# Two transformer blocks in one program: the indexer's matmuls interleaved with the projections, relu kept in PSUM, a row sum in another form, and some fillers and weight roundings moved

## The reference

```python
# first block: one input projection, then two attentions
h = rmsnorm(x, g_pre);  proj = h @ w_in        # qa ka va gate_a qi ki wi qb kb vb fb gate_b
# [indexer] scores of all keys, 128 best kept per query
dots  = einsum('bqhd,bsd->bqhs', qi, ki)
score = einsum('bqhs,bqh->bqs', relu(dots), wi)          # 8 heads, causal mask
_, sel = top_k(score, 128)
# [dsa] softmax attention of qa over the selected keys ka, va
# [fox] attention of qb over kb, vb with a bias from cumsum(log_sigmoid(fb)), causal
out = (sigmoid(h @ w_merge)_a * (att_a*silu(gate_a)) @ w_branch_a
     + sigmoid(h @ w_merge)_b * (att_b*silu(gate_b)) @ w_branch_b) @ w_out
x = x + rmsnorm(out);  x = x + rmsnorm(sigmoid(x @ w_ple_gate) * (p @ w_ple))
# second block
# [swa] 8 heads, 2 kv heads, window of 128 keys, a sink in the denominator:
m = maximum(max(s), sink);  p = exp(s - m);  denom = sum(p) + exp(sink - m)
# [mla] latent attention: q from a 384-wide latent (w_uq), k and v from a 256-wide one (w_ukv)
x = x + (sigmoid(g_a)*(o_a @ w_o_swa) + sigmoid(g_b)*(o_b @ w_o_mla)) @ w_out
x = x + (silu(h @ w_gate) * (h @ w_up)) @ w_down;  return rmsnorm(x)
```

## Time and profile before

| | us |
|---|---|
| median of three runs (lowest, highest) | 1259.21 (1259.14, 1259.68) |
| the profiled execution, its own time | 1259.51 |
| its span in the trace | 1257.7 |
| PE busy | 1206.5 (96%) |
| DVE busy | 636.8 (51%) |
| ACT busy | 540.8 (43%) |
| POOL busy | 532.8 (42%) |
| mean granted clock of PE | 0.989 |

### The profile page before, as it was taken

The page is one execution under the profiler, slowest core; times in us unless marked ns, Lnnn a source line. Parts: engine busy times, 40 slices in busy tenths (PEclk is TensorE's granted clock), DMA queues, the critical chain, the costliest instruction groups (busy, mean ns, idle before and its releaser), DMA issues.

```text
span 1257.7 us, 15767 instructions
## 1 busy us (share of the span) xinstructions
PE 1206.5 (96%) x5874; PEld 1000.5 (80%) x5874; DVE 636.8 (51%) x1484; ACT 540.8 (43%) x967; POOL 532.8 (42%) x284
## 2 busy tenths in 40 slices
PE   9989899999999989699988999999999999999997
PEld 8868678788888878499877777788788888888886
DVE  5499575684537274874874585763412222230003
ACT  6443573476523354445763476423432222231112
POOL 1436554344443434134252585444244444424441
PEclk9999999999999999799999999999999999999999
DMA  8303662302322422133112301423323232323221
GB/s 265 101 1 118 172 180 68 101 1 77 119 91 93 144 99 99 34 137 120 34 39 67 101 1 35 174 94 102 99 90 111 69 106 94 101 101 112 84 89 67
DMA packets 71114, 119.18 MB, mean 95 GB/s; under 512 B 5624, under 2 KB 33144, under 8 KB 70656
## 3 DMA queue, kind: packets, MB, share of 16 engines
q1 hardware_dynamic: 71040, 118.19, 28.8%
HBM read 107.67 MB, written 4.21 MB: 89 GB/s over the span
## 4 chain that ended last, share of the span: by engine, by line
PE 80%; DVE 10%; issue 3%; ACT 3%; POOL 2%; SPq 1%; DMA 1%; DVEq 0%; ACTq 0%; POOLq 0%
PE bank L1607 61%; PE bank L1890 9%; PE bank L1688 2%; PE bank L1656 2%; PE bank L1732 2%; DVE sc L1334 2%; PE bank L1670 2%; DVE m L1330 2%; PE bank L1632 1%; DVE tmp L1396 1%; DMA w_raw<-in_w_in 1%; POOL w_lo L652 1%; POOL w_lo L669 1%; SPq L585 1%; SPq L586 0%
## 5 line engine op out<-in xcount | busy, mean ns | idle before, releaser
L652 POOL TENSOR_TENSOR w_lo<-w_raw,w_hi 128x2048 fp32r<-128x2048 f32 (+4 forms) x87 | 383.8, 4412 | 600.6 <-ACT w_hi L737 565.5
L1607 PE MATMUL bank<-aH,w_hi 128*128 128x512 f32 x800 | 318.6, 398 | 9.9 <-DVE aL L1408 3.9
L1607 PE MATMUL bank<-aH,w_lo 128*128 128x512 f32 x800 | 312.9, 391 | 0.0
L1607 PE MATMUL bank<-aL,w_hi 128*128 128x512 f32 x800 | 312.6, 391 | 0.0
L737 ACT ACTIVATE w_hi<-w_raw 128x2048 fp32r<-128x2048 f32 (+4 forms) x83 | 151.8, 1828 | 270.9 <-PE bank L1607 173.7
L1607 PEld LDWEIGHTS bank<-aH,w_hi 128*128 128x128 f32 x800 | 151.1, 189 | 40.7 <-issue 11.5
L1607 PEld LDWEIGHTS bank<-aH,w_lo 128*128 128x128 f32 x800 | 150.4, 188 | 32.5
L1607 PEld LDWEIGHTS bank<-aL,w_hi 128*128 128x128 f32 x800 | 151.0, 189 | 26.4
L1607 PE MATMUL bank<-w_hi,aH 128*128 128x512 f32 (+4 forms) x224 | 78.1, 349 | 6.9 <-ACT aH L971 6.6
L1086 DVE TENSOR_TENSOR fg<-bank,rB 128x512 f32<-128x512 f32 x22 | 15.1, 691 | 127.2 <-PE bank L1607 127.2
L1607 PE MATMUL bank<-w_lo,aH 128*128 128x512 f32 (+4 forms) x224 | 76.4, 341 | 0.0
(11 more groups left out here) (309 smaller groups left out, 2125.8 us busy)
## 6 DMA issues: line engine op xcount, KB each, us to landing
w_raw<-in_w_in SPq DMA_DIRECT2D x23, 1024.0 KB, 5.1
w_raw<-in_w_gate SPq DMA_DIRECT2D x22, 512.0 KB, 4.0
w_raw<-in_w_up SPq DMA_DIRECT2D x22, 512.0 KB, 4.9
w_raw<-in_w_down SPq DMA_DIRECT2D x11, 1024.0 KB, 4.8
w_raw<-in_w_merge SPq DMA_DIRECT2D x8, 1024.0 KB, 4.8
w_raw<-in_w_out SPq DMA_DIRECT2D x8, 1024.0 KB, 5.1
w_raw<-in_w_ple_gate SPq DMA_DIRECT2D x4, 1024.0 KB, 4.9
fK<-kbT SPq DMA_DIRECT2D x24, 128.0 KB, 2.7
```

What stands on the lines that cost most here:

```text
L652: pool.tensor_tensor(out=w_lo[:, c % 2, 0:n], in0=w_raw[:, c % 2, 0:n], in1=w_hi[:, c % 2, 0:n].bitcast(F32), op=ALU.subtract).then_inc(w_ ...
L1607: ins = pe.matmul(o, l, r, start=(kk == 0 and m == 0), stop=(kk == total - 1 and m == 2), skip_group_check=True)
```

## The change

Six edits.

1. PE: the second half of `qb` is interleaved with the ten transposed tiles (three tiles, then one tile of `qb`, and so on), and the first half of `kb` with the 24 indexer pieces (one side step of three matmuls after every three pieces, eight more after the last). ACT and DVE split `qi` before the rest of `sm` and the forget gate, so that the sources of the tiles are there. The cumulative sum is drained before the rounding of `vb`.
2. Relu is written back into the bank that it reads, and DVE's multiply-add reads the bank; the drain of a bank is now signalled by DVE. The first head adds the causal mask in the same instruction, and the three separate adds go.
3. Rounds: 2, then the dsa keys' drain, then 7, then one before each half of `vb`'s drain, 2 after fox, 3 later (16 as before; 11 before fox in place of 10).
4. fox's odd pairs get places of their own (`oddQ`, `oddK`). Pairs 0 and 1 are both split before fox on DVE; POOL does pair 1's low part before `ga`'s second chunk. Pairs 2 and 3 are split at units 6 and 14, on DVE and POOL alike.
5. swa's add of the sink to the row sum is `tensor_scalar` with the sum as a scalar operand in place of `tensor_tensor`.
6. swa's extra fillers start at unit 35 and no longer at 32, and the two halves of the rounding of `uq0` are done at units 36 and 37 and no longer at 38 and 39.

```diff
-SIDE_ALL, SIDE_FROM, SIDE_NEXT = 32, 2, 38
+SIDE_ALL, SIDE_FROM = 32, 2
+SIDE_NEXT = {"fox": 38, "dsa": 38, "swa": 36, "mla": 38}
-SIDE_TAIL = {..., "swa": ((25, 1), (32, 2)), "mla": ((22, 1),)}
+SIDE_TAIL = {..., "swa": ((25, 1), (35, 2)), "mla": ((22, 1),)}
-PAIR_HI_AT, PAIR_LO_AT = {1: 1, 5: 2, 13: 3}, {0: 1, 3: 2, 11: 3}
-ROUNDS_FIRST, ROUNDS_NEXT = 10, 3
+PAIR_HI_AT, PAIR_LO_AT = {6: 2, 14: 3}, {6: 2, 14: 3}
+ROUNDS_KA, ROUNDS_PAIR, ROUNDS_VB, ROUNDS_NEXT = 2, 7, 1, 2
...
+        oddQ, oddK = place("oddQ", 123, [P, S]), place("oddK", 125, [P, S])
...
-            return ((tQ, tK)[part][:, :], (qbT, kbT)[part][:, 0, :], (tQ, tK)[part][:, :], (qbT, kbT)[part][:, 1, :])[j].bitcast(F32R)
+            return ((tQ, tK), (oddQ, oddK))[j % 2][part][:, :].bitcast(F32R)
...
 # ACT
-            for b in range(NB):
+            for b in range(2):
                 evac("sm", b, ...)
+            split_high(tmI, spI, 1)
+            for b in range(2, NB):
+                evac("sm", b, ...)
+            hi_through(UNITS["sm"][0] + UNITS["sm"][1] + 1)
...
-                if i >= RING:
-                    act.wait_ge(idx_done, i - RING + 1)
                 wait_filled(act, "idx", i)
-                empties(act.activation(sp[:, i % RING, 0:nk], bank_of("idx", i)[:, 0:nk], ACT.Relu), "idx", i)
+                act.activation(dots, dots, ACT.Relu).then_inc(relued, 1)
+            hi_through(UNITS["kb"][0] + 1)
+            evac("cum", 0, cT[:, :], src=bank_of("cum", 0)[0:H, :], scale=-8.0)
             ahead("kb")
-            evac("cum", 0, cT[:, :], src=bank_of("cum", 0)[0:H, :], scale=-8.0)
...
 # DVE, swa
-                            link(dve.tensor_tensor(out=sums[:, c], in0=sums[:, c], in1=rsum[:, c], op=ALU.add))
+                            link(dve.tensor_scalar(sums[:, c], sums[:, c], rsum[:, c], None, ALU.add))
...
 # DVE, split_pair: only pairs 2 and 3 wait for copies
-                if j:
+                if j >= 2:
                     for h in range(2):
-                        dve.wait_ge(head_landed[h], 96 * (2 if j == 3 else 1))
+                        dve.wait_ge(head_landed[h], 96 * (j - 1))
...
 # DVE, indexer
-                if h == 0:
-                    dve.tensor_scalar(sc[:, lo:hi], dve_in, w, None, ALU.mult).then_inc(idx_done, 1)
-                else:
-                    dve.wait_ge(idx_done, i - 2)
-                    dve.scalar_tensor_tensor(out=sc[:, lo:hi], in0=dve_in, scalar=w, in1=sc[:, lo:hi],
-                                             op0=ALU.mult, op1=ALU.add).then_inc(idx_done, 1)
-            for b in range(1, NB):
-                ins = dve.tensor_tensor(out=sc[:, hi - P:hi], in0=sc[:, hi - P:hi], in1=tab("causal")[:, 3 * P:4 * P], op=ALU.add)
+                dve.wait_ge(relued, i + 1)
+                if h:
+                    wait_emptied(dve, "idx", i - 3)
+                empties(dve.scalar_tensor_tensor(out=sc[:, lo:hi], in0=bank_of("idx", i)[:, 0:hi - lo], scalar=w,
+                                                 in1=sc[:, lo:hi] if h else tab("causal")[:, (3 - b) * P:4 * P],
+                                                 op0=ALU.mult, op1=ALU.add), "idx", i)
...
 # PE
-            gemm("qb", aH, aL, False)
...
-            for j in range(H):
-                turn_tile("t.qi", j, lambda b: spI[:, b, j, :].bitcast(F32))
+            for j in range(NB):
+                for t in range(3 * j, min(3 * j + 3, H)):
+                    turn_tile("t.qi", t, lambda b: spI[:, b, t, :].bitcast(F32))
...
+                part("qb", first + 1, j, aH, aL, False, None, 0, 0, CHUNKS[first + 1][0])
...
+                if i % 3 == 2:
+                    kb(i // 3, i // 3 + 1)
+            kb(8, 16)
```

67 lines of the change are left out of this document (39 added, 28 removed).

## The result

The changed kernel takes 1245.49 us in the median of four runs (1244.98 to 1248.60), the kernel before 1259.45 beside it; the ratio is 0.9892, 95% interval 0.9874 to 0.9910. Run again in a later comparison it took 1246.47 (six runs) against 1258.31, ratio 0.9905 (0.9888 to 0.9923). So it is 12 to 14 us faster, and 1246.5 was forecast. The profiled executions are 1259.51 and 1245.50, spans 1257.7 and 1243.6: 14.1 apart.

A forecast was written before the change was run, and what follows sets the result against it. The prediction took PE to bound the kernel (80% of the chain of waits, busy for 96%). Its terms, 3.4 + 2.4 + 0 + 1.5 + 5.4 = 12.7, came off 1259.5, less 0.3: 1246.5 us, range 1241.5 to 1252.

The forecast's parts named there:

- Turned tiles, 4.3: Ten transposed tiles before the scores: mixed among `qb`'s matmuls they cost 4.6 us instead of 8.87, gain 4.3.
- Scores, 0.2 - 1.1: Indexer scores mixed with `kb`: 9.8 us against 9.97, gain 0.2, less 1.1 for a new wait near the fifth piece.
- Start of fox, 2.4: fox's first units: PE's waits of 1.43 for POOL's scaling and 0.92 for head 2's key DMA go, gain 2.4.
- Drains of `vb`, 0: Before fox: `vb`'s drains stand behind a DVE round each, but DVE is some 10 us ahead, so 0.
- Behind fox, 0: PE's 1.75 wait for `spA` stays: rope adds start earlier but end under the same POOL subtraction, gain 0.
- Row sum, 1.5: swa's row sum as `tensor_scalar` is no longer held while POOL subtracts, so PE's waits shrink, gain 1.5.
- The rival by the port rule: swa's row sum stays blocked as `tensor_scalar`, since DVE shares a port pair with GpSimd; then 1248 us, chance 0.12.
- End of swa, 5.4: PE behind swa's last output: idle stretches of 1.67 and 2.27 go (3.9), plus 1.5 from the clock, gain 5.4.
- the interleaving does what it says: The rival denied this: late sources of `t.qi` make PE stand inside `qb`, 1.9 less gain, 1248.5 us, chance 0.05.
- The start-up wait: Rival: the new wait in the scores is hidden and drains come sooner too; about 1241.5 us, chance 0.12.
- the end of swa gave all of its idle time, not half: Rival: swa's end gives half, 2.7 and not 5.4 us; then 1249.2, chance 0.2.
- Relu in the bank slow: Indexer scores: at 1.16 us a relu the kernel is no longer faster, at 1.5 it takes 1267 us; chance 0.04.

The follow-up runs named there:

- relu to SBUF: The changed kernel with relu written to the five-deep ring in SBUF again and DVE reading it there: 1244.69 us against 1259.34 for the kernel before.
- kb whole: The changed kernel with the first half of `kb` behind the score pieces and the cumulative sum, as before: 1250.85 us against 1259.34 for the kernel before.
- pair 0 first: The kernel before with two of the ten rounds moved behind pair 0's cast, one ahead of each half of `vb`'s drains: 1258.47 us against 1258.31.
- the experiment with one round: The changed kernel with one round directly after fox in place of two, and four later in place of three: 1245.63 us against 1258.31 for the kernel before.
- the fillers alone: The kernel before with swa's extra fillers starting at unit 35, the rounding of `uq0` left at units 38 and 39: 1255.22 us against 1259.38.
- the first block alone: The changed kernel with swa's row sum, fillers and rounding put back as before: 1251.43 us against 1259.38 for the kernel before.

## Why the prediction was right, step by step

- **The total.** That both medians lie within 1 us of the forecast is in part luck. By stretch the profiles give 1.3 more than forecast up to fox, 0.7 less from there to dsa and 0.5 more from swa on; and of the 12.7 in the sum 1.5 was for a fall of the clock that the kernel before shows in some executions only.
- **Turned tiles, 4.3.** Measured 8.87 - 4.5 = 4.3. Right in size; 1.9 of it is due to the early split of the queries, which I had counted only as a condition.
- **Scores, 0.2 - 1.1.** Measured 1.0 - 0.95. The wait at the fifth piece came as forecast. The term that was mis-sized is the switch between score pieces and `kb`: I took 0.2 a round from the side step of fox, where it goes to small transposes, and it measured 0.05 (1.75 - 1.02 - 0.68).
- **That the two edits stand in one term** hid what each does: relu in the bank loses 1.2 (relu to SBUF), and without `kb` between the pieces it loses about 4 (kb whole).
- **Start of fox, 2.4.** Measured 2.4 (PE is 4.7 earlier at fox's first row and 7.1 at head 2's), but the cause that I named, pair 1's place, has 1.0 of it. The 1.43 was there because pair 0's cast came late and pair 1's cast waited for the copies of head 1; a wait of 0.29 for the maximum went with it, and 0.68 stayed for the copies of head 2. Edit 4 alone in the kernel before would take that cast's wait away too; this was not run, so how the two edits share the 1.4 stays open. The table has 1.7 for the whole stretch, since the wait of 0.98 takes 0.9 back and 0.25 comes behind fox.
- **Drains of `vb`, 0.** Measured 0 in the changed kernel. The 1.65 that PE waits for them in "pair 0 first" comes from a held cast, so no run says what the two rounds among the drains cost by themselves. A round takes 3.2 us (204.77 to 207.99), twice the 1.6 that the forecast has beside the mask adds; its "3 us less" behind fox is right.
- **Behind fox, 0.** Measured 0.25. The mechanism, the start under the same subtraction, is seen in the 5.17 us, and the experiment with one round shows where it ends.
- **Row sum, 1.5.** Measured 1.6 alone. The rival by the port rule fell.
- **End of swa, 5.4.** Idle 3.9, as forecast, by the fillers alone. The other 1.6 to 1.9 is the clock and is true of the two profiles only, as the last section shows; the median of the run with the fillers alone is 4.2 faster.
- **What was left out:** the new wait of 0.98 is chance and lowers the gain of this profile. And the idle stretches of the turned tiles, 1.38 and 1.93 before the scores, are the ones behind which the clock most often fell in the kernels that have them; that they go was not in my sum. Whether this is a part of the 8 us that the first block alone gained in the runs stays open: the mean granted clock is 0.9894 over its five runs and 0.9888 over the 28 of the kernel before, a difference within their scatter.
- **The other rivals.** PE has no idle stretch between 51.02 and 66.46, so the interleaving does what it says. The start-up wait was not hidden (0.95), and the end of swa gave all of its idle time, not half.
- **Relu in the bank slow (the rival on the other side).** A relu took 364 to 582 ns, at the longest half of the 1.16 from which it would have decided. The 0.53 that the forecast sets as the most for one relu was a mean: to SBUF the longest took 698 ns (L881). What the rival says of the bank being held through relu and DVE's pass is so, at 1.2 us here.

## What to carry over

Of a change with several edits, price each against the kernel with the others in it: relu in the bank cost 1.2 us beside the mixing and about 4 without it, and rounds moved behind the pair gained nothing in the kernel before, where a cast slid under POOL's subtraction. Where an idle time names an engine, ask what that engine's own chain waited for before crediting the edit that touches its order. And an operation that POOL's subtraction will hold is best put in front of it: in the traces a start three microseconds sooner against the subtraction gained 0.25, and 0.9 more gained the rest.
